# Expert weights in quarters of matrices instead of halves: one transformer block pair on one core

## What is computed

```
g_idx = argmax(h @ w_rg + b_rg)                     # one of 4 groups
top_v, top_i = top_k(e_sel, 2)                      # two of 8 experts in the group, 32 experts in all
gate  = p_group * softmax(top_v)
y     = (silu(x @ w_g[e]) * (x @ w_u[e])) @ w_d[e]  # w_g, w_u: 1024 x 512, w_d: 512 x 1024
out   = sum over the two chosen experts of gate * y
```

## Time and profile before

| What | Value |
|---|---|
| median of three runs | 1540.02 us (1537.84 to 1541.22) |
| profiled execution, device time | 1537.69 us |
| its span from first to last instruction | 1535.5 us |
| mean granted TensorE clock | 0.977 of full speed |
| TensorE matmul busy | 1426.6 us, 93% |
| DMA queue 1 (SP) | 312.63 MB |

### The profile page before, as it was taken

How to read it: one execution, slowest core, us unless ns; L and a number is a source line. 1 busy time by engine, 2 the same in 40 slices (tenths; PEclk the granted TensorE clock), 3 DMA queues, 4 the chain that set the end, 5 groups by cost and what they waited for, 6 DMA issues and landing times. The chain is left out here.

```text
span 1535.5 us, 17397 instructions
## 1 busy us (share of the span) xinstructions
PE 1426.6 (93%) x6990; PEld 976.0 (64%) x6990; DVE 801.0 (52%) x1311; ACT 463.8 (30%) x671; POOL 31.7 (2%) x59
## 2 busy tenths in 40 slices
PE   6999999999949999999989997999897999999996
PEld 5889777787844434343334333787575888888884
DVE  5899987766334323233223325567667434343446
ACT  4432356672320000010000012335536323132333
POOL 0000000000010000000000000000000000000000
PEclk9999999999979999999999998999998999999998
DMA  9441344543958999999999994441012322323301
GB/s 347 150 165 56 103 162 168 180 154 122 371 224 356 419 419 419 419 420 418 419 420 419 419 419 145 146 137 56 28 57 81 95 97 90 102 95 96 106 5 55
DMA packets 113078, 328.51 MB, mean 214 GB/s; under 512 B 5240, under 2 KB 72952, under 8 KB 87536
## 3 DMA queue, kind: packets, MB, share of 16 engines
q1 hardware_dynamic: 108336, 312.63, 53.5%
q0 software_dynamic: 4096, 12.81, 2.5%
q10 hardware_dynamic: 576, 2.10, 0.3%
HBM read 327.23 MB, written 4.21 MB: 216 GB/s over the span
## 5 line engine op out<-in xcount | busy, mean ns | idle before, releaser
L2572 PE MATMUL second_bank<-second_cx_lo,second_c_hi 128*128 128x512 f32 x352 | 140.8, 400 | 15.1 <-DVE second_cx_lo L2255 8.2
L1652 DVE SCALAR_TENSOR_TENSOR x_mid<-moe_bank,mod_col,x_mid 128x512 f32<-128x512 f32 x136 | 91.3, 744 | 96.6 <-PE moe_bank L1736 96.4
L2573 PE MATMUL second_bank<-second_cx_hi,second_c_lo 128*128 128x512 f32 x352 | 138.8, 394 | 0.0
L2574 PE MATMUL second_bank<-second_cx_hi,second_c_hi 128*128 128x512 f32 x352 | 138.8, 394 | 0.0
L2092 ACT ACTIVATE second_c_hi<-second_c_raw 128x2048 fp32r<-128x2048 f32 x43 | 82.1, 1910 | 159.4 <-PE second_bank L2574 159.4
L2572 PE MATMUL second_bank<-g_lo,second_c_hi 128*128 128x512 f32 x320 | 127.3, 398 | 0.0
L2574 PE MATMUL second_bank<-g_hi,second_c_hi 128*128 128x512 f32 x320 | 124.7, 390 | 0.0
L2573 PE MATMUL second_bank<-g_hi,second_c_lo 128*128 128x512 f32 x320 | 124.7, 390 | 0.0
L2239 DVE TENSOR_TENSOR second_c_lo<-second_c_raw,second_c_hi 128x2048 fp32r<-128x2048 f32 x43 | 98.5, 2291 | 39.5 <-ACT second_c_hi L2092 39.5
L1643 DVE SCALAR_TENSOR_TENSOR moe_y_lo<-moe_bank,moe_slot_gate,g_lo 128x512 fp32r<-128x512 f32 x32 | 22.6, 747 | 135.3 <-ACT g_lo L1486 135.3
L2572 PEld LDWEIGHTS second_bank<-second_cx_lo,second_c_hi 128*128 128x128 f32 x352 | 67.3, 191 | 33.5 <-issue 12.2
(11 more groups left out here) (458 smaller groups left out, 2694.5 us busy)
## 6 DMA issues: line engine op xcount, KB each, us to landing
second_c_raw<-in_w_mlp_dram SPq DMA_DIRECT2D x32, 1024.0 KB, 5.3
moe_weights<-in_w_exp_gate_dram SPq DMA_DIRECT2D x12, 2048.0 KB, 27.5
moe_weights<-in_w_exp_up_dram SPq DMA_DIRECT2D x11, 2048.0 KB, 25.9
moe_weights<-in_w_exp_down_dram SPq DMA_DIRECT2D x10, 2048.0 KB, 27.0
stream<-in_w_in_dram SPq DMA_DIRECT2D x18, 1024.0 KB, 5.7
stream<-in_w_mod_t_dram SPq DMA_DIRECT2D x16, 1024.0 KB, 5.0
spare<-in_w_exp_up_dram SPq DMA_DIRECT2D x6, 2048.0 KB, 27.8
kq<-in_w_exp_down_dram SPq DMA_DIRECT2D x6, 2048.0 KB, 29.3
```

What stands on the lines that cost most here:

```text
L1652: dve.scalar_tensor_tensor(out=x_mid[:, c, :], in0=bank[F_BANK[c % 4]][:], scalar=mod_col[:, 40 + c:41 + c], in1=x_mid[:, c, :], op0=ALU.m ...
L2572: pe.matmul(out, a_hi, b_lo, start=first, stop=False)
L2573: pe.matmul(out, a_lo, b_hi, start=False, stop=False)
L2574: return pe.matmul(out, a_hi, b_hi, start=False, stop=last)
```

## The change

Each 2 MB unit becomes two transfers of 1 MB in two buffers of 128 x 2048 floats. There are 18 buffers, and a block has 12 steps: four quarters each of gate, up and down. Each partition now reads one run of 4 KB for each expert. TensorE waits for and frees each quarter by itself, 8 matmul instructions per quarter; the order of the matmuls stays the same. The memory used stays the same, and `h2_rows` now lies over the last two buffers, 16 and 17. Two neighbouring buffers share one `free` semaphore. The waits of `mixer_stage` are moved with their units (n 8 and n 10), the waits of ScalarE and VectorE name the last quarter of a matrix (j 3, 7, 11).

```diff
-SLOTS = 9
-EARLY = 6
+SLOTS = 18
+EARLY = 12
 BLOCKS = N_EXPERTS // 2
-STEPS = 6 * BLOCKS
+STEPS = 12 * BLOCKS
...
-    return [spare[:, 0:4096], kq[:, 0:4096], vals[:, 0:4096], work[:, 0:4096], stream[:], split[:]]
+    return [t[:, 2048 * i:2048 * i + 2048] for t in (spare, kq, vals, work, stream, split) for i in range(2)]
...
-                             src[0].rearrange("e (p h k) f -> h p e (k f)", p=P, h=2)[n % 2, :, 0:2, :])\
+                             src[0].rearrange("e (p h k) f -> h p e (k f)", p=P, h=4)[n % 4, :, 0:2, :])\
...
-                if n == 4:
+                if n == 8:
                     sp.wait_ge(lo_done, NS)
-                if n == 5:
+                if n == 10:
                     sp.wait_ge(acc_ready, first_tile[NS - 1])
...
-            [sb(f"weights{i}", [P, 4096])[:] for i in range(SLOTS - EARLY)]
+            [sb(f"weights{i}", [P, 2048])[:] for i in range(4)]
+        with nc.sbuf_tensor("moe_rows", [P, 4096], F32) as staged:
+            pass
+        slots += [sb(f"weights{i}", [P, 2048])[:] for i in range(4, 6)]
...
-        free = [sem(f"weights_free{i}") for i in range(SLOTS)]
+        free = [sem(f"weights_free{i}") for i in range(SLOTS // 2)]
...
-        PARTS = [(wg, 0), (wg, 1), (wu, 0), (wu, 1), (wd, 0), (wd, 1)]
+        PARTS = [(src, h) for src in (wg, wu, wd) for h in range(4)]
...
-                if s == SLOTS - 1:
+                if s == SLOTS - 2:
                     sp.wait_ge(h2_stored, 16 * TC)
                 if s >= SLOTS:
-                    sp.wait_ge(free[s % SLOTS], times_used(s, n_late))
+                    sp.wait_ge(free[s % SLOTS // 2], 2 * times_used(s, n_late) + (s % 2 - 1))
...
-                act_e.wait_ge(*done(at, 1))
+                act_e.wait_ge(*done(at, 3))
...
-                act_e.wait_ge(*done(at, 5))
+                act_e.wait_ge(*done(at, 11))
...
-                dve.wait_ge(*done(at, 3))
+                dve.wait_ge(*done(at, 7))
...
-                for k in range(4):
-                    c = 4 * h + k
+                for k in range(2):
+                    c = 2 * h + k
...
-                    if j < 2:
-                        pe.wait_ge(x_done, 2 * no + (j + 1))
-                    if j == 2 and (i is not None or b):
+                    if j in (0, 2):
+                        pe.wait_ge(x_done, 2 * no + (j // 2 + 1))
+                    if j == 4 and (i is not None or b):
...
                     pe.wait_ge(landed[q], 16 * uses + 16)
-                    if j < 4:
-                        hidden_half(bank[2 + j // 2], q, j % 2, n_experts).then_inc(free[q], 1)
+                    if j < 8:
+                        hidden_part(bank[2 + j // 4], q, j % 4, n_experts).then_inc(free[q // 2], 1)
                     else:
-                        down_half(q, j % 2, n_experts).then_inc(free[q], 1)
+                        down_part(q, j % 4, n_experts).then_inc(free[q // 2], 1)
```

More of the change, by code:

```diff
@@ L352, in first_experts @@
             def first_experts(n):
-                src = (w["w_exp_gate"], w["w_exp_up"], w["w_exp_down"])[n // 2]
+                src = (w["w_exp_gate"], w["w_exp_up"], w["w_exp_down"])[n // 4]
                 sp.dma_start(expert_slots(spare, flex, vals, kq, stream, split)[n].rearrange("p (e n) -> p e n", e=2),
-                             src[0].rearrange("e (p h k) f -> h p e (k f)", p=P, h=2)[n % 2, :, 0:2, :])\
+                             src[0].rearrange("e (p h k) f -> h p e (k f)", p=P, h=4)[n % 4, :, 0:2, :])\
                   .then_inc(expert_landed[n], 16)
@@ L1223, in moe_stage @@
         a_t = part([P, 4, 128])
-        h2_rows = slots[SLOTS - 1].rearrange("p (t d) -> p t d", t=TC)
+        h2_rows = staged[:].rearrange("p (t d) -> p t d", t=TC)
         xs = work[:, 4096:8192].rearrange("p (c t) -> p c t", c=KC)
@@ L1320, in moe_stage @@
         f_used = sem("f_used")
-        wg = w["w_exp_gate"][0].rearrange("e (p h k) f -> h p e (k f)", p=P, h=2)
-        wu = w["w_exp_up"][0].rearrange("e (p h k) f -> h p e (k f)", p=P, h=2)
-        wd = w["w_exp_down"][0].rearrange("e (p h k) d -> h p e (k d)", p=P, h=2)
-        PARTS = [(wg, 0), (wg, 1), (wu, 0), (wu, 1), (wd, 0), (wd, 1)]
+        wg = w["w_exp_gate"][0].rearrange("e (p h k) f -> h p e (k f)", p=P, h=4)
+        wu = w["w_exp_up"][0].rearrange("e (p h k) f -> h p e (k f)", p=P, h=4)
+        wd = w["w_exp_down"][0].rearrange("e (p h k) d -> h p e (k d)", p=P, h=4)
+        PARTS = [(src, h) for src in (wg, wu, wd) for h in range(4)]
         F_BANK = (0, 1, 4, 5)
         AFTER = BEFORE + 1
-        ALL_STEPS = STEPS + 6
-        late_set = [(6 * BEFORE + j) % SLOTS for j in range(6)]
+        ALL_STEPS = STEPS + 12
+        late_set = [(12 * BEFORE + j) % SLOTS for j in range(12)]
         def step_of(b, j):
-            return 6 * b + j if b < BEFORE else 6 * (b + 1) + j
+            return 12 * b + j if b < BEFORE else 12 * (b + 1) + j
         def times_used(s, n_late):
-            if s >= 6 * AFTER and s % SLOTS in late_set:
+            if s >= 12 * AFTER and s % SLOTS in late_set:
                 return n_late + (s // SLOTS - 1)
@@ L1346, in done @@
             if i is not None:
-                s = 6 * BEFORE + j
-                return free[s % SLOTS], i + (s // SLOTS + 1)
+                s = 12 * BEFORE + j
+                return free[s % SLOTS // 2], 2 * i + (2 * (s // SLOTS) + s % 2 + 1)
             s = step_of(b, j)
-            return free[s % SLOTS], times_used(s, n_late) + 1
+            return free[s % SLOTS // 2], 2 * times_used(s, n_late) + (s % 2 + 1)
         def gate_column(at):
@@ L1380, in _ @@
             for b in range(BEFORE):
-                for j in range(6):
-                    if 6 * b + j >= EARLY:
+                for j in range(12):
+                    if 12 * b + j >= EARLY:
                         weights(b, j, None)
@@ L1388, in _ @@
                 for j, (src, h) in enumerate(PARTS):
-                    s = 6 * BEFORE + j
-                    sp.wait_ge(free[s % SLOTS], i + s // SLOTS)
-                    sp.dma_start(slots[s % SLOTS][:, 0:2048].rearrange("p (e n) -> p e n", e=1),
+                    s = 12 * BEFORE + j
+                    sp.wait_ge(free[s % SLOTS // 2], 2 * i + (2 * (s // SLOTS) + s % 2 - 1))
+                    sp.dma_start(slots[s % SLOTS][:, 0:1024].rearrange("p (e n) -> p e n", e=1),
                                  src[h, :, bass.ds(e, 1), :]).then_inc(landed[s % SLOTS], 16)
             for b in range(BEFORE, BLOCKS):
-                for j in range(6):
+                for j in range(12):
                     weights(b, j, n_late)
-            last = max(s for s in range(ALL_STEPS) if s % SLOTS == 3)
-            sp.wait_ge(free[3], times_used(last, n_late) + 1)
+            last = max(s for s in range(ALL_STEPS) if s % SLOTS == 7)
+            sp.wait_ge(free[3], 2 * times_used(last, n_late) + 2)
             sp.dma_start(work[:, 2048:4096].rearrange("p (k n) -> p k n", k=KC),
@@ L1759, in transpose_act, with hidden_part @@
                 ins.then_inc(at_ready, 1)
-            def hidden_half(out, slot_no, h, n_experts):
-                parts = slots[slot_no].rearrange("p (e k f) -> p e k f", e=2, k=4)
+            def hidden_part(out, slot_no, h, n_experts):
+                parts = slots[slot_no].rearrange("p (e k f) -> p e k f", e=2, k=2)
                 m = P // n_experts
-                for k in range(4):
-                    c = 4 * h + k
+                for k in range(2):
+                    c = 2 * h + k
                     for e in range(n_experts):
@@ L1770, in hidden_half, with down_part @@
                 return ins
-            def down_half(slot_no, h, n_experts):
-                parts = slots[slot_no].rearrange("p (e k d) -> p e k d", e=2, k=2)
+            def down_part(slot_no, h, n_experts):
+                parts = slots[slot_no].rearrange("p (e d) -> p e d", e=2)
                 m = P // n_experts
[L1776 to L1781, removed]
+                for half in range(2):
+                    for e in range(n_experts):
+                        ins = pe.matmul(bank[6 + half][m * e:m * e + m, :], a_t[:, h, m * e:m * e + m],
+                                        parts[:, e, 512 * half:512 * half + 512], start=(h == 0), stop=(h == 3))
                 return ins
@@ L1802, in block_of @@
                         results(b - 1 if i is None and n_late is None else (i + (BEFORE - 1) if i is not None else n_late + (b - 1)))
-                    if j == 4:
+                    if j == 8:
                         if i is not None or b:
```

## The result

The changed kernel takes 1543.27 us, median of 20 runs (1539.68 to 1547.07); the kernel before takes 1538.74 us in 20 runs beside it. The ratio is 1.0025 (95% interval 1.0019 to 1.0031): slower by 3 to 5 us (4.5 between the medians), where +3.6 was forecast. The profiled execution has a span of 1541.8 us and a time of 1544.1.

The account below looks back on a forecast made before the run. DMA was taken to bound the experts' stage up to TensorE's start on unit 67, TensorE all that follows. Terms 8.7 - 2.2 - 1.7 - 1.2 = +3.6 us gave 1543.5 us, range 1535.5 to 1550.

Parts of the forecast that it names:

- Step (1): Experts' weight stream: runs of 4 KB instead of 8 KB cost e = 0.147 us per unit, +8.7 us over 59 units.
- A: Rival: small packets cost nothing in the experts' stage, e = 0, only the gains stay: 1534.9 us; chance 15%.
- B: Rival: HBM likes the strided 4 KB runs less, e = 0.25, the end binds too: +10.7 us, 1550.7; chance 17%.
- Rival C: The loss is absorbed, with e near 0.09 or the stores' gain at 3 us: 1541 us; chance 17%.
- Step (2): Start of the experts' stream: TensorE frees the first buffer after one quarter, so DMA restarts sooner: -2.2 us.
- Step (3): At the binding point TensorE starts on a quarter, so only the last quarter is left after its landing: -1.7 us.
- Step (4): Tokens' stores before the first gather get half the engines beside 4 KB weight packets, not a third: -1.2 us.
- (5): Twice as many issues on SP and six more waits per block on TensorE: priced at nothing.
- (6): Stage's end, block 15: slack shrinks by 5.7 of 7.4 us, not binding; it binds from e = 0.21.
- the rate came: Sign in the profile after: a DMA rate near 407 to 410 GB/s from 500 to 790 us.

Follow-up runs that it names:

- E3: Kernel before with the late turn after block 7 instead of block 11: 1533.22 us, ratio 0.9952.
- E1: Kernel before with the changed kernel's transfers (two of 1 MB per unit, 4 KB runs) into the old nine buffers, without the finer grain: 1545.19 us, ratio 1.0035.
- E2: Kernel before with two transfers of 1 MB per unit, one for each expert, but runs of 8 KB: 1539.09 us, ratio 0.9996.
- E6: Kernel before, but TensorE signals after block 0's first quarter and SP then issues unit 9 in two 1 MB transfers: 1538.43 us, ratio 0.9997.
- E5: Kernel before with the gate halves of blocks 9 to 11 in two 1 MB transfers each, TensorE starting on the first: 1539.15 us, ratio 1.0002.
- E7: Changed kernel with the late turn after block 7 instead of block 11: 1542.68 us, ratio 1.0022 against the kernel before.
- E4: Kernel before, but SP waits for the tokens' stores before unit 6, not before unit 8: 1535.84 us, ratio 0.9973.
- E10: Kernel before with the late turn after block 7, and units 6 to 8 issued only after tokens' stores and first gather have landed: 1532.38 us, ratio 0.9954.

## Why the prediction was right, step by step

**What bounds the kernel** was read rightly. E3 moved nothing but the place where DMA and TensorE meet and won 5.6 us; E1 changed only how the bytes are fetched and moved rate and time together; E2 changed the number of transfers and moved neither.

**Step (1)**, the term that decides, held: 2.097 / 0.408 = 5.140 us per unit against 5.005, so e = 0.135 where 0.147 was forecast, and over 59 units +8.0 us against 8.7; the trace shows +8.4 between the two fixed points. The Trainium skill, "DMA: Bandwidth & Descriptors", section "iDMA fabric", gives 408.7 GB/s for one load stream with 4 KB rows in 1 MB transfers; the 408 GB/s of the stage agree. Rivals A and B fall: the cost is neither hidden nor raised by the 16 KB between runs, for the stretch with neighbouring runs had 407. Rival C falls with them: e was not near 0.09, and the stores' gain was under 1 us.

**Step (2)** failed as a mechanism. It took the first freed buffer for what starts the stream; E6 shows that DMA then lacks the second. In the changed kernel the first issue came 32.9 us after the stage's start instead of 33.8, with a clock that was low for longer, but at 42 us queue 1 had moved 9.15 MB against 8.98, a lead of 0.17 MB or 0.4 us. E1, which frees whole halves only and so lacks step (2), had its first issue at 32.8 us and was further ahead, 9.33 MB. So no gain of step (2) shows, where 2.2 us were forecast; the little that there is goes with step (4).

**Step (3)** held in the changed kernel: the stretch after the last landing is 1.7 us shorter, as forecast. E5 had nothing of it to show by itself.

**Step (4)** was the right mechanism and too large. Queues 1 and 10 from 444 to 446 us, before and after:

```profile
q1 hardware_dynamic: 73, 0.60, 70.5%
q10 hardware_dynamic: 70, 0.26, 32.0%
```

```profile
q1 hardware_dynamic: 112, 0.46, 55.6%
q10 hardware_dynamic: 110, 0.39, 47.2%
```

The stores do get nearly half instead of nearly a third, as sharing by packet would have it: the two queues moved the same number of packets, 73 and 70, then 112 and 110. The Trainium skill, "DMA: Bandwidth & Descriptors", "Queues, rings and completion order", says that an engine goes round its queues packet by packet; the trace agrees in the even counts. A packet on that page is a group of typically 9 to 17 descriptors, while the packets of the profile are single runs of 4 or 8 KB, and they come out even already in half a microsecond (16 and 17 from 444.0 to 444.5 us, on 16 engines).

From 9 to 15 us after the stage's start the stores moved 0.75 MB before and 1.21 MB after. But before, queue 1 was done at 16 us and left the engines to the stores (0.60 MB from 448 to 450 us), so that they caught up: at 17 us 1.77 of their 2.10 MB were moved before, 2.00 after, and at 18 us all in both. The prediction had counted this end too, with 2.6 MB left in queue 1 when the stores began; it was 2.5. What else made the gain smaller is open. The first gather came 19.1 us after the stage's start instead of 19.3: 0.2 us, not 1.2. E1 and E7 fetch in the same runs; their gathers came at 18.7 and 19.1 us. TensorE's first expert matmul, at 29.4 us before and between 29.3 and 29.5 in the profiles of E2, E3, E5 and E6, came at 29.1 us in the changed kernel, 28.6 in E1 and 28.8 in E7. So the step is worth about 0.5 us, 0.3 to 0.8. The large gain beside it, taking the weights out of the stores' way (E4), was in the rows and not seen.

**Steps (5) and (6)** held: no price for issues (E2) or boundaries (two quarters run through in 3.65 us, at 786.92 above, as a half did), and no wait for weights after the late turn in the changed kernel. Of the signs that the prediction named, the rate came, and the waits from block 8 on, at 7.9 us just under the 8 to 12 named; SP's first issue at 462 us and the first gather a microsecond sooner did not.

So the mechanism that decides was right, and the forecast's +3.6 came out near the measured +4 to +4.5 in part by luck. Of the gains of (2) and (4), 3.4 us, some 0.5 was there, and step (1) cost 0.7 less. By the terms as measured, 8.0 - 1.7 - 0.5, the sum is +5.8 us, above the medians' 4.5 and their interval of 3 to 5. That 1543.5 was named and 1543.3 measured is luck too: the three runs it started from had a median 1.3 us above that of the 20 later ones.

For E1 the account closes. Its profile has a length 6.3 us above that of the kernel before, close to the medians' 6.4. SP's first issue into a freed buffer, TensorE on unit 67, and block 11's second down half, with the stage's start at 433.13 us:

```profile
465.95 0.88 SPq L1380 DMA_DIRECT2D spare<-in_w_exp_up_dram  x2
...
780.45 3.65 PE L1772 MATMUL moe_bank<-stream,work 128*64 128x512 f32 x16 [1.47 <-DMA stream<-in_w_exp_gate_dram]
...
802.33 3.65 PE L1784 MATMUL moe_bank<-moe_weights,spare 128*64 128x512 f32 x16 [0.91 <-DMA moe_weights<-in_w_exp_down_dram]
```

The first issue comes 1.0 us sooner, from there to unit 67 it takes 7.8 us more (314.5 against 306.7), and in block 11's down halves a new wait of 0.9 us stands against the 1.7 us of the fallen clock, which this execution doesn't have there.

For the changed kernel the length is 5.6 us more, close to the terms' 5.8. The microsecond between this and the medians' 4.5 is about what its profile's slower first half took (5.44 against 4.34 us); that this is the reason is not shown.

## What to carry to other kernels

Where the DMA queue is full, count bytes per contiguous run, not transfers: twice the transfers with the same run cost nothing, half the run cost 2.6% of the rate, and that cost grows with each unit up to the last point where the other engine waits. Where two engines are nearly level, look first at where they meet (a turn that needs fewer bytes, moved to an earlier place, won 5.6 us) and at small transfers on the critical path that share the engines with a prefetch nobody waits for yet (3 us). A lead at the start of a stream can be gone after the next buffer if that one doesn't come sooner too (E6).

## What the runs showed of the hardware

The rate of a full queue followed the run: 408 GB/s with 4 KB, 419 with 8 KB, 426 with 16 KB. In time per 2 MB on each of the 16 engines, these are 5.140, 5.005 and 4.923 us for 32, 16 and 8 packets: 16 packets fewer save 0.135 us, 8 fewer 0.082, so by this estimate a packet costs 8 to 10 ns beside its bytes, here with a full queue. (Twice the completion writes, E2, didn't change the rate.)

The four 512 KB stores landed in 2.6 us each (median) when alone (E4), and in 10.7 us beside 4 MB of weights; the first gather kept TensorE waiting for about 4 us after its issue alone (E10: issued at 446.96, transposes at 451.31), 8 us beside a prefetch (450.94 to 459.10 in the kernel before).

TensorE's granted clock at the same place in the program differs between executions: at the boundary of two stages the same 8 matmuls took 1.05 or 1.87 us, and block 0's first half 4.2 (E1, E6) to 5.8 us (E5). In the pair above this came to 2.3 us, more than some of the steps weighed here, and so the steps are better compared from a fixed point of the same trace.
